# One-element ScalarE activations ahead of six functions, in a two-block transformer kernel on one core

## The reference

```python
h = rmsnorm(x, n1) * (1 + sc1) + sh1            # norms: mean of squares, square root
q, k, v, gb, gcv, u, ga, gv = split_proj(h @ w_in)
y_attn = windowed_attention(q, k, v, kc, vc, sink) @ w_attn_out      # exp
x = x + g1 * merge_branches(y_attn, y_conv, ga, gv, w_mix_out)       # sigmoid
h2 = rmsnorm(x, n2) * (1 + sc2) + sh2
# peer: for each token 8 heads choose 16 of 16384 experts each
g = softmax(best)                                                     # exp
act = gelu(einsum('thkd,td->thk', u_tab[idx], h2))                    # gelu
x = x + g2 * einsum('thk,thkd->td', g * act, v_tab[idx])
```

```python
u = conv_b + sum(conv_w[j] * shifted(h @ w_up, j) for j in range(3))
gate, val = split(u)
x = x + (silu(gate) * val) @ w_down                                   # silu
```

## Time and profile before

| what | value |
|---|---|
| timed runs | 1576.19, 1578.48, 1580.05 us (median 1578.48) |
| profiled execution: span | 1577.9 us; its own time isn't given beside it |
| PE busy | 1413.4 us (90%) |
| ACT busy | 777.4 us (49%) |
| DVE busy | 1074.8 us (68%) |
| table loads, all lines | 48, of 1283 ns each |

### The profile page before, as it was taken

The page is one execution under the profiler, slowest core; times in us unless marked ns, Lnnn a source line. Parts: engine busy times, 40 slices in busy tenths (PEclk is TensorE's granted clock), DMA queues, the critical chain, the costliest instruction groups (busy, mean ns, idle before and its releaser), DMA issues.

```text
span 1577.9 us, 21891 instructions
## 1 busy us (share of the span) xinstructions
PE 1413.4 (90%) x7816; PEld 1042.8 (66%) x7816; DVE 1074.8 (68%) x2270; ACT 777.4 (49%) x1649; POOL 295.1 (19%) x296
## 2 busy tenths in 40 slices
PE   7999988899998778778778889998999998999998
PEld 3889987544453223223222278998999987989997
DVE  4678665766666667766665578547777775477776
ACT  3655542444444444444444364746555566455555
POOL 0001100444454444434344300000000010000000
PEclk9999998999999999999999999999999999999999
DMA  9456755999999999999999944234555531245553
GB/s 398 177 204 224 249 175 211 372 418 427 427 426 427 427 427 426 427 426 427 427 427 426 428 186 154 106 108 161 183 175 179 182 127 61 94 167 184 188 186 130
DMA packets 62586, 432.91 MB, mean 274 GB/s; under 512 B 7073, under 2 KB 7585, under 8 KB 12193
## 3 DMA queue, kind: packets, MB, share of 16 engines
q0 software_dynamic: 41616, 285.76, 43.7%
q1 hardware_dynamic: 20160, 145.37, 26.0%
q10 hardware_dynamic: 720, 0.62, 0.1%
HBM read 430.67 MB, written 1.05 MB: 274 GB/s over the span
## 4 chain that ended last, share of the span: by engine, by line
PE 61%; DMA 19%; ACT 9%; DVE 8%; issue 2%; POOL 0%; ACTq 0%; DVEq 0%; POOLq 0%
PE banks L668 26%; PE banks L1059 15%; DMA arena<-in_peer_uv,experts 11%; DMA tok_b<-in_peer_uv,experts 4%; PE banks L1227 3%; PE banks L1195 3%; PE banks L705 3%; DVE wlow L1746 3%; ACT diag L1515 2%; PE banks L864 2%; PE banks L905 2%; PE banks L766 1%; ACT whigh L1271 1%; PE banks L824 1%; PE banks L845 1%
## 5 line engine op out<-in xcount | busy, mean ns | idle before, releaser
L1059 PE MATMUL banks<-arena,diag 128*128 128x512 f32 x780 | 382.9, 624 | 84.9 <-ACT diag L1515 84.9
L1746 DVE TENSOR_TENSOR wlow<-wring,whigh 128x1024 fp32r<-128x1024 f32 x234 | 276.0, 1221 | 121.5 <-ACT whigh L1271 121.4
L2190 DVE CUSTOM_DVE_ANT_0 arena<-arena,scores 128x1024 f32<-128x1024 f32 x200 | 245.2, 1226 | 162.5 <-DMA arena<-in_peer_uv,experts 160.5
L1059 PEld LDWEIGHTS banks<-arena,diag 128*128 128x128 f32 x780 | 140.2, 193 | 315.7 <-ACT diag L1515 191.5
L1271 ACT ACTIVATE whigh<-wring 128x1024 fp32r<-128x1024 f32 x234 | 234.6, 1050 | 97.6 <-DMA wring<-in_w_down 34.3
L1695 POOL DMA_INDIRECT arena<-in_peer_uv,experts x200 | 210.5, 1052 | 314.8 <-PE banks L1059 264.6
L668 PE MATMUL banks<-f_high,whigh 128*128 128x256 f32 x720 | 205.2, 285 | 8.0 <-DVE wlow L1746 5.5
L668 PE MATMUL banks<-f_low,whigh 128*128 128x256 f32 x720 | 203.7, 283 | 0.0
L668 PE MATMUL banks<-f_high,wlow 128*128 128x256 f32 x720 | 203.7, 283 | 0.0
L1507 ACT ACTIVATE dots<-dots 128x1 f32<-128x1 f32 x256 | 51.9, 203 | 302.3 <-DVE dots L2190 302.0
L668 PE MATMUL banks<-a_high,whigh 128*128 128x256 f32 x528 | 159.3, 302 | 11.8 <-DVE a_low L1792 6.0
(11 more groups left out here) (275 smaller groups left out, 2411.1 us busy)
## 6 DMA issues: line engine op xcount, KB each, us to landing
wring<-in_w_up SPq DMA_DIRECT2D x44, 1024.0 KB, 4.9
wring<-in_w_down SPq DMA_DIRECT2D x22, 1024.0 KB, 4.9
wring<-in_w_in SPq DMA_DIRECT2D x17, 1024.0 KB, 5.4
wring<-in_w_qkv_a SPq DMA_DIRECT2D x12, 1024.0 KB, 4.9
arena<-in_w_mod SPq DMA_DIRECT2D x8, 1024.0 KB, 15.6
arena<-in_w_mod_t POOLq DMA_DIRECT2D x16, 512.0 KB, 5.3
hT<-in_w_mod_t POOLq DMA_DIRECT2D x16, 512.0 KB, 4.7
wring<-in_peer_w_q SPq DMA_DIRECT2D x5, 1024.0 KB, 4.8
```

The costliest lines, as they stand in the source:

```text
L1059: mm = nc.tensor.matmul(banks[:, 2 + 2 * b + half, :], diag[:, n % DIAGS, :], ring[ROW_PLACE[n]][:, D + half * 512:D + (half + 1) * 512], ...
L1746: V.tensor_tensor(low, w, high.bitcast(F32), ALU.subtract).then_inc(w_split, 1)
L2190: V.tensor_tensor_reduce(out=ring[ROW_PLACE[n]][:, 0:D], in0=ring[ROW_PLACE[n]][:, 0:D], in1=h2tok[:, b, :], scale=1.0, scalar=0.0, op0=AL ...
```

## The change

A new tensor `table_cell` of one fp32 element in each partition is declared between `sin2` and `csil`. A function `tables_for` runs one activation of a given function from a constant into it; nobody reads it. It is called at five places of the code, the last of which runs once in each of two layers: six activations. Everything else stays as it is.

```diff
--- before.py
+++ after.py
@@ -219,6 +219,7 @@
         sinks = sb("sinks", [P, 24])[:, :]
         cos2 = sb("cos2", [P, T])
         sin2 = sb("sin2", [P, T])
+        table_cell = sb("table_cell", [P, 1])
         csil = sb("csil", [P, KT, 2])
         mod = sb("mod", [P, MOD_TILES, 2])
         mod_row = sb("mod_row", [2, 2, WIDE])
@@ -1306,6 +1307,9 @@
                 nc.scalar.activation(root[:, norm % 2, :], norm_bank(norm), ACT.Sqrt,
                                      bias=const[:, C_EPS:C_EPS + 1]).then_inc(norm_root, 1)
 
+            def tables_for(function):
+                nc.scalar.activation(table_cell[:, :], const[:, C_EPS:C_EPS + 1], function)
+
             def square_x(norm):
                 square(xT, x_part, 0, dst=x_squares)
                 sqrt(norm)
@@ -1466,7 +1470,9 @@
                         copy(a_high[:, pair, :], merged[:, pair, :]).then_inc(merge_rounded, 1)
                     round_next()
             round_next()
+            tables_for(ACT.Sqrt)
             square_x(2)
+            tables_for(ACT.Exp)
             shift(hT, 2 * KT, 3, 0)
 
             def scores_out(h):
@@ -1498,6 +1504,7 @@
                     h2_out(g)
                 if h == 1:
                     weights_of(0)
+                    tables_for(ACT.Gelu)
 
             def spread(n):
 
@@ -1611,6 +1619,7 @@
                 round_weights(value["slot"], KT, value["landed"], only=(1,))
                 square(xT, x_part, 8 + 8 * l)
                 sqrt(5 + 2 * l)
+                tables_for(ACT.Silu)
                 f0, fill, slots = l * FF_STEPS, ffn_plan[l]["fills"], ffn_plan[l]["slots"]
                 bias0 = V_CONVB + l * 2 * FF_TILES
                 tap0 = V_CONVW + (l * CONV_W + 2) * 2 * FF_TILES
```

## The result

The changed kernel takes 1589.12 us (1588.09 to 1589.88, 4 runs) against 1578.4 us (1576.19 to 1580.05, 4 runs): ratio 1.0063, 95% interval 1.0049 to 1.0077. It is slower, by 10.7 us, outside the forecast range. The profiled execution has a span of 1586.8 us (before: 1577.9). L numbers in its rows are shifted by the added lines: the added activation is L1311, the root L1307, the Gelu L1514, the Silu L1650, the gather L1704.

A forecast was written before the change was run, and what follows sets the result against it. DMA was taken to bound the expert gather (282 to 920 us), mostly PE ahead of and behind it. Gains of 0.4 us (Gelu) and 0.8 us (Silu), others 0, took 1578.5 to 1577.3 us; range 1574.4 to 1581.0.

The forecast's parts named there:

- Slower through addresses: Rival, chance 0.09: the new cell moves nearly all tensors 32 bytes off alignment, slowing the gather; 1584 us and more.
- the 0.74%: Loss of DMA rate in the gather from which moved addresses would cost over 4.7 us and decide the result.
- my bound of 41 us: Price of moved addresses if the gather's 638 us ran at the poorest full-share rate, 401 GB/s against 427.
- a pair of DVE products: Evidence against an address cost: DVE took 0.42 us into a tile 32 bytes off, 0.43 us into an aligned one.
- The estimate of 2.5 us: Gather: from the Trainium skill's rule, one extra 32-byte beat on each 8 KB row, 0.4%, 2.5 us.
- Root of norm 2: Square root's table load moved from 250.62 to 238.0 us: hidden before and after, 0 us.
- Exponential: First exponential's load moved from 277.92 to 252.65 us, 0.84 us of cover left before the shift: 0 us.
- the drain: Rival, chance 0.05: a table switch at 252.65 takes 2.2 us or more, the shift is 0.5 us late; 1577.8 us.
- Gelu: First expert rows: Gelu and PE 1.28 us sooner, filling idle DMA time between 304 and 312 us; gain 0.4 us.
- Root of norm 3: Load moved from 937.41 to 922.4 us into ACT's idle time; nothing on the chain waits for it, 0 us.
- Silu: Both layers' FFN: load ahead of first Silu gone, PE's wait for the weight difference shorter; 0.40 us each, 0.80 in all.
- the granted clock: Rival, chance 0.06: a shorter PE gap keeps its clock up at the first expert rows, 7.2 us gained; 1571.3 us.

The follow-up runs named there:

- cell_no_calls: Kernel before with only the new cell declared where the change has it, no activation called: 1591.18 us against 1580.13, ratio 1.0066.
- filler_128: Kernel before with everything from gain1 on (weight ring, arena, row tiles) 128 bytes higher: ratio 1.0059.
- filler_256: Kernel before with everything from gain1 on (weight ring, arena, row tiles) 256 bytes higher: ratio 0.9991.
- filler_32: Kernel before with everything from gain1 on (weight ring, arena, row tiles) 32 bytes higher: ratio 1.0061.
- tok_on_32: Kernel before with tok_a, tok_b (slots of 56 of the 256 gathered rows) and the small tiles behind them 32 bytes higher: ratio 1.0000.
- ring_only_32: Kernel before with weight ring and rounded weights 32 bytes higher, the arena and all behind it 512 bytes higher: ratio 0.9948.
- calls_cell_last: Changed kernel, all six activations kept, with the new cell declared behind every other tensor so no address moves: 1577.32 us, ratio 0.9973.

## Why the prediction was wrong

**The step that failed** is the rival "Slower through addresses": the forecast took 0 us for the moved addresses and gave the rival a chance of 0.09, and the runs show about 11 us there (cell_no_calls: 1591.18 against 1580.13, without a single activation). The place was right (the gather's 638 us), and so was the mechanism, slots that start 32 bytes past a multiple of 512, though the boundary is one of 256. The measured loss of rate, 7 of 427 GB/s or 1.6%, is past the 0.74% from which I had said it decides, and the price lies under my bound of 41 us. The only evidence against the rival was a pair of DVE products. DVE is another engine than the one at stake, and the pair says nothing of a transfer, as the text half admits. With no row for or against it, and the stretch that DMA bounds at stake, there was no reason to put the term at nothing; a chance of a third and a range up to 1590 would have been honest.

The Trainium skill's rule ("DMA: Bandwidth & Descriptors", "How a descriptor splits into AXI transactions") names the boundary that the runs show, 256 bytes (filler_128 and filler_256), though it speaks of what a transaction reads, and here it is the place written to that was moved. Its price doesn't fit. The estimate of 2.5 us from one beat for each row was a quarter of what the runs show; more bytes ahead of the start should cost more beats, and the gather of filler_128 is 2.6 us shorter than that of filler_32; and a row doesn't pay by itself, as tok_on_32 shows.

**Point by point, the rest.** Root of norm 2: hidden at both ends, as said. Exponential: 0.82 us of cover were left, 0.84 forecast; the drain that the Trainium skill counts ("ScalarE: Activation LUTs", "What ACT_TABLE_LOAD costs") did not appear: load, activation and next square stand edge to edge at 239.64, 240.93 and 241.04. Gelu: 1.8 us earlier on ACT and on PE (1.28 forecast; the copy ahead of it ran 0.3 us earlier too), the DMA shares at 1.01 as forecast, and worth nothing that could be told: the term of 0.4 us was read off idle time of one execution, most of which the next one did not have. Root of norm 3: hidden. Silu: 0.47 us in each layer instead of 0.40; the mechanism held, and with Silu early DVE waited for neither it nor the weights. The forecast gain of 1.2 us is, without the shift, some 0.9 by the traces. The times don't resolve it: against the kernel before beside each, the activations change the ratio from 1.0066 to 1.0063 in the changed kernel's placement, from 0.9995 to 0.9978 with the arena 256 bytes up, and from 0.9948 to 0.9963 in ring_only_32's, with intervals of 0.0014 to 0.0024 to either side; calls_cell_last by itself has 0.9973 (0.9953 to 0.9993). Of the other rivals, the granted clock stayed partly up (0.69 instead of 0.50 between 290 and 292 us), and no gain at the end followed from it: the DMA was at a share near 1 there, as held against that rival.

## What to carry to other kernels

A declaration is a change too: a scratch cell placed ahead of the big tiles moves them all, and here 4 bytes in a partition cost some ten times what the instructions that use it gained. Declare small tensors last, or check the starts of what DMA writes at its full rate against multiples of 256 bytes. Try other distances between the weights and the moving operand of long rows of matmuls, too: two of the placements tried were faster than the kernel before, though neither was meant to be. When two changes of a microsecond or two are compared, compare each with a run of the kernel before beside it. Before hiding a table load, see whether the compiler's load stands ahead of the wait already; four of these six activations moved a load that cost nothing that could be told where it was.

## What the runs showed of the hardware

A full-rate gather of 8 KB rows runs at 427 GB/s into slots that start at multiples of 256 bytes and at 420 to 421 into slots 32, 64 or 128 bytes past one, with the transfer engines' busy share at 1.01 in both. It takes a stream mostly of such rows: with 22% of them the rate stays at 427, with 78% it falls to 422 and some 7 us of the 11 are lost.

A matmul of 256 moving columns took 120 ns from start to start in the kernel before, and, by product, 116 to 119 ns where its moving operand lay 32 or 480 bytes further from its weights: 848 to 852 instead of 836 in 100 us, at a granted clock of 1.00 in both. 256 bytes changed nothing. And a table load (1.28 us), the activation behind it and the next instruction stand edge to edge on ACT.
